# First up-projection panel of two convolution feed-forward layers: both tiles interleaved per plane, or one tile after the other

## The reference

```python
def conv_gated_ffn(h, w_up, conv_w, conv_b, w_down):
    a = h @ w_up                                   # 1024 -> 2 * 2816
    ap = jnp.pad(a, ((0, 0), (1, 1), (0, 0)))
    a = ap[:, :-2] * conv_w[0] + ap[:, 1:-1] * conv_w[1] + ap[:, 2:] * conv_w[2] + conv_b
    gate, val = a[..., :D_FF], a[..., D_FF:]
    return (jax.nn.silu(gate) * val) @ w_down

# in second_block, for l in range(2):
    x = x + memory_cross_attention(h, mem, ...)    # "mem"; its output product is followed by
    h = rms_norm_2(x, ffn_norm[l])                 # this norm, and then by
    x = x + conv_gated_ffn(h, ffn_w_up[l], ffn_conv_w[l], ffn_conv_b[l], ffn_w_down[l])   # "ffnc"
```

## Time and profile before

| | |
|---|---|
| median of 3 runs | 3700.81 us (3695.28 to 3701.74) |
| the profiled execution | 3697.01 us, its span 3695.2 us |
| PE busy | 3520.4 us, 95% of the span |
| DVE, ACT, POOL busy | 54%, 40%, 1% |
| chain that ended last | PE 87%, DVE 7%, ACT 2%, DMA 1% |

### The profile page before, as it was taken

How to read it: one execution, slowest core, us unless ns; L and a number is a source line. 1 busy time by engine, 2 the same in 40 slices (tenths; PEclk the granted TensorE clock), 3 DMA queues, 4 the chain that set the end, 5 groups by cost and what they waited for, 6 DMA issues and landing times.

```text
span 3695.2 us, 54759 instructions
## 1 busy us (share of the span) xinstructions
PE 3520.4 (95%) x21540; PEld 2923.2 (79%) x21540; DVE 1977.4 (54%) x2724; ACT 1474.0 (40%) x2212; POOL 20.6 (1%) x38
## 2 busy tenths in 40 slices
PE   7999995799999999999999999999999998989998
PEld 6888775678887888897778888778788896778887
DVE  4442469854434443335754424856677348557753
ACT  3332432243323332335643324655444247454432
POOL 0000000000000000000000000000000000000000
PEclk9999996699999999999999999999999999999999
DMA  3223220022232223222022233012233330222232
GB/s 121 96 95 97 77 74 9 2 80 96 96 94 83 96 96 96 82 91 75 18 80 96 95 97 93 30 40 83 90 100 94 96 97 13 69 81 91 96 98 90
DMA packets 84098, 296.08 MB, mean 80 GB/s; under 512 B 9504, under 2 KB 9504, under 8 KB 83680
## 3 DMA queue, kind: packets, MB, share of 16 engines
q1 hardware_dynamic: 82512, 288.24, 24.4%
q0 software_dynamic: 1424, 5.51, 0.5%
HBM read 291.61 MB, written 2.10 MB: 79 GB/s over the span
## 4 chain that ended last, share of the span: by engine, by line
PE 87%; DVE 7%; ACT 2%; issue 2%; DMA 1%; SPq 0%; DVEq 0%; ACTq 0%
PE PS L254 22%; PE PS L245 22%; PE PS L246 22%; PE PS L343 2%; PE PS L346 2%; PE PS L344 2%; PE PS L996 2%; PE PS L1007 1%; PE PS L1020 1%; PE PS L377 1%; DVE H_LO L470 1%; DVE WK L2556 1%; DVE WLO L221 1%; ACT WHI L217 1%; PE PS L384 1%
## 5 line engine op out<-in xcount | busy, mean ns | idle before, releaser
L245 PE MATMUL PS<-WK_R,WHI 128*128 128x512 f32 (+1 forms) x3680 | 1430.6, 389 | 16.4 <-DVE WLO L221 7.5
L246 PE MATMUL PS<-WK_R,WLO 128*128 128x512 f32 (+1 forms) x3680 | 1425.0, 388 | 0.0
L221 DVE TENSOR_TENSOR WLO<-RAW,WHI 128x1024 fp32r<-128x1024 f32 x563 | 689.0, 1224 | 1203.2 <-ACT WHI L217 1200.6
L217 ACT ACTIVATE WHI<-RAW 128x1024 fp32r<-128x1024 f32 x563 | 596.0, 1059 | 997.2 <-PE PS L254 822.3
L245 PEld LDWEIGHTS PS<-WK_R,WHI 128*128 128x128 f32 x3680 | 692.5, 188 | 168.6 <-issue 23.3
L246 PEld LDWEIGHTS PS<-WK_R,WLO 128*128 128x128 f32 x3680 | 692.5, 188 | 140.7 <-issue 0.7
L254 PE MATMUL PS<-H_LO,WHI 128*128 128x512 f32 x2680 | 673.1, 391 | 4.7 <-DVE H_LO L470 4.5
L254 PEld LDWEIGHTS PS<-H_LO,WHI 128*128 128x128 f32 x2680 | 502.0, 188 | 118.3 <-DVE H_LO L470 15.9
L254 PE MATMUL PS<-HID_LO,WHI 128*128 128x512 f32 x1056 | 263.2, 389 | 0.0
L254 PEld LDWEIGHTS PS<-HID_LO,WHI 128*128 128x128 f32 x1056 | 197.9, 188 | 40.9
L1188 DVE SCALAR_TENSOR_TENSOR SC<-SC,VEC 128x511 f32<-128x511 f32 x176 | 132.2, 751 | 110.5 <-ACT SC L1155 98.6
(11 more groups left out here) (378 smaller groups left out, 3559.0 us busy)
## 6 DMA issues: line engine op xcount, KB each, us to landing
RAW<-in_ffn_gu SPq DMA_DIRECT2D x176, 512.0 KB, 3.4
RAW<-in_f_up SPq DMA_DIRECT2D x88, 512.0 KB, 3.6
RAW<-in_ffn_dn SPq DMA_DIRECT2D x64, 512.0 KB, 3.5
RAW<-in_c_in SPq DMA_DIRECT2D x32, 512.0 KB, 3.4
RAW<-in_f_dn SPq DMA_DIRECT2D x32, 512.0 KB, 3.5
RAW<-in_ffn_dn SPq DMA_DIRECT2D x32, 384.0 KB, 3.1
RAW<-in_a_in SPq DMA_DIRECT2D x22, 512.0 KB, 3.5
RAW<-in_b_out SPq DMA_DIRECT2D x16, 512.0 KB, 3.6
```

The costliest lines, as they stand in the source:

```text
L217: nc.scalar.activation(WHI[:, slot, :], RAW[:, slot, :], ACT.Copy).then_inc(S("w_hi"), 1)
L221: nc.vector.tensor_tensor(WLO[:, slot, :], RAW[:, slot, :], WHI[:, slot, :].bitcast(F32), ALU.subtract).then_inc(S("w_lo"), 1)
L245: pe.matmul(o, WHI[:, slot, w], hi(k), start=(first and b_ == 0), stop=False)
L246: pe.matmul(o, WLO[:, slot, w], hi(k), start=False, stop=False)
```

## The change

For an early layer with two tiles, first_tiles now does the high products tile by tile. feature_hi of tile 0 waits for tile 0's weights alone and then for each plane. Both norm sums follow, and then feature_hi of tile 1 with its own wait. The low products and the spread behind them are as before. For all other calls nothing changes. The number of PE instructions is the same (6891 rows in both orders), and the queues of ACT, DVE, POOL and SP are the same.

```diff
             pe_bank(pe, p)
             apart = late(n)
-            pe.wait_ge(S("w_lo"), p.N + tiles)
-            for k in range(DT):
+            by_tile = early(n) and tiles > 1
+            if by_tile:
+                for i in range(tiles):
+                    feature_hi(pe, p, i, h_hi, range(DT), True, i, fresh=h_fresh(n))
+                    if i == 0:
+                        norm_add(pe, p, n, DT - 2)
+                        norm_add(pe, p, n, DT - 1)
+            else:
+                pe.wait_ge(S("w_lo"), p.N + tiles)
+            for k in () if by_tile else range(DT):
                 w = slice(128 * k, 128 * k + 128)
                 pe.wait_ge(S("norm_hi"), DT * n + k + 1)
                 for i in range(tiles):
```

## The result

The changed kernel took 3683.12 us, the median of 5 runs (3679.90 to 3685.41). The kernel before took 3700.81 us (5 runs, 3695.28 to 3703.41). The ratio is 0.9955, with a 95% interval of 0.9943 to 0.9966. So it is faster by 0.45%, some 17 us. 3683.5 us was predicted, with a range of 3677 to 3690.

What follows compares the result with a forecast made beforehand. The prediction took PE, busy 95% of the span, as the bound. Its terms of 9.44, 5.29 and 2.59 us sum to 17.32 us, taking the median of 3700.81 us to 3683.5 us, range 3677 to 3690 us.

Steps and rivals of the forecast that it cites:

- Start: First matmul at both seams: PE waits for tile 0's piece alone, 4.72 us earlier at each, 9.44 us.
- Clock: High products at both seams: with the gap short, PE stays at full clock, saving 2.76 and 2.53 us, 5.29 us.
- gap of 1.30 us: Idle time ahead of mem's output product: its window kept a clock of 1.00, the nearest row for the 5.29 us.
- Rival 1: Tile 0's start: the clock falls all the same, 12.0 us saved, 3688.8 us (one seam: 3686); chance 0.12.
- Low products: Tile 0's eight low products: earlier sum frees the reciprocal, so 1.82 us instead of 3.11 and 3.12, 2.59 us; chance not given.
- the covers: Slack before PE wants its operands: plane 7 1.3 us, tile 1's piece 0.7 us, low planes 0.5 us.
- Rival 3: Whole program: no change within 7.4 us, perhaps by second-layer mixb losing its clock, at most 1.7 us a window; chance 0.05.
- Rival 2: After tile 0's early start: PE stands before tile 1's piece or the low planes, 12.7 us left, 3688; chance 0.07.
- rival 4: Ahead of tile 1: late square of plane 7 and running sum hold PE up, slower, 3708.2 us or more; chance 0.02.

Runs made afterwards that it cites:

- wait for both: Changed kernel, but PE waits for both tiles' weights before tile 0's first product, as before the change; 3697.46 us against 3701.12 before, ratio 0.9993.
- busy gap: Kernel before, plus five unused products filling PE's gap ahead of its wait in the two layers; 3696.72 us against 3701.12 before, ratio 0.9993.
- sums late: Changed kernel, but both norm sums stand behind the high products of both tiles; 3689.69 us against 3701.12 before, ratio 0.9973.
- one seam: Changed kernel, with the new order in the first of the two layers only; 3693.36 us against 3700.59 before, ratio 0.9981.
- all layers: Changed kernel, with the four other feed-forwards' first panels tile by tile too, their sums unmoved; 3690.86 us against 3700.59 before, ratio 0.9973.
- late start: Changed kernel, but PE waits for the last plane's square before tile 0's first product; 3692.03 us against 3701.12 before, ratio 0.9982.
- reciprocal last: Kernel before, with VectorE's reciprocal behind all eight low planes at the two seams, not the fifth; 3699.98 us against 3700.23 before, ratio 0.9997.
- late, busy gap: Changed kernel with PE waiting for the last plane's square before tile 0, plus three unused products ahead; 3690.88 us against 3700.23 before, ratio 0.9972.

## Why the prediction was right

**Start.** 9.44 us were predicted and 9.99 measured: gaps of 0.39 and 0.63 us instead of 5.74 and 5.27. Waiting for both tiles brings the gap back, 5.07 us at the first seam. The forecast gaps were 1.02 and 0.55 us. The second was met. At the first, the odd execution is that of the kernel before, not that of the changed one: its ScalarE waited 1.91 us for tile 0's piece, where the wait is 1.27 us in the changed kernel and 1.24 us in "wait for both":

```profile
2594.85 1.06 ACT L217 ACTIVATE WHI<-RAW 128x1024 fp32r<-128x1024 f32 x1 [1.24 <-DMA RAW<-in_f_up]
```

The other kernels with an early start have first gaps of 0.27 to 0.37 us. So the 4.72 us a seam of the forecast are the repeatable term, and the 0.55 us above them are the late load of one execution, which is no gain of the change.

**Clock.** 5.29 us were predicted. The 32 high products took 7.47 and 7.44 us after, against 9.12 + 1.01 and 8.89 + 1.01 us before, so 2.66 + 2.46 = 5.12 us were saved. The busy gap shows it alone, and the windows show 1.00 through both seams. The forecast had only one gap of 1.30 us to go by, and gave the fall a chance of 0.12. The clock held at all seven early starts of four profiles (changed, "sums late", "one seam", "all layers"), behind gaps of 0.27 to 0.64 us. Rival 1 didn't come true at the gaps that were left (0.39 and 0.63 us). It would have at gaps of 3 us, as the late start shows: the row of 1.30 us was the right one to go by, but no proof for gaps much longer.

**Low products.** 2.59 us were predicted and 2.61 measured (1.81 us at each seam, from 3.11 and 3.12). Sums late brings the stall back, and reciprocal last removes it in the kernel before. The step's reason is shown, not only its size.

**Sums.** Not in the sum: both groups in a row take 1.70 us, where they took 1.61 apart (0.80 + 0.81). The forecast had the 1.7 us in its times of the covers, but left the difference out of the sum. That costs 0.18 us in all.

**Sum.** 9.99 + 5.12 + 2.61 - 0.18 = 17.54 us, which is what the seams give (9.22 + 8.32). The forecast was 17.32. Without the 0.55 us of the late load it is 17.0. That the total is met so closely is in part luck, since the interval of the ratio alone reaches from 12.6 to 21.1 us. But each term is met within 0.2 us, the late load apart, and that isn't luck. The span is 17.1 us shorter. The stretch ahead of the first seam was 1.17 us shorter in this execution, that between the seams 1.61 us longer, and that behind the second seam equal to 0.01 us.

**Rival 3 in small.** The 1.61 us are the clock further on, as the rival had it. Two windows of the second mixb were at full clock before and at half after. The first two rows are one place of mixb before and after, the windows are the changed kernel's:

```profile
3066.95 1.15 PE L1757 MATMUL PS<-CON,HID 128*96 128x128 f32 x8 [2.69 <-DVE HID_LO L2056]
...
3056.56 1.77 PE L1765 MATMUL PS<-CON,HID 128*96 128x128 f32 x8 [2.69 <-DVE HID_LO L2064]
...
3056.70:3060.10 3.40, 3.40 (x18) 3.34 (x17) 2.81 (x5) 1.49 (x3) 0.00 (x0) 0.50 0.02 5
3070.40:3073.80 3.40, 3.37 (x14) 2.39 (x14) 3.36 (x7) 1.43 (x4) 0.00 (x0) 0.50 0.00 0
```

The changed kernel is 10.39 us ahead at this place and 8.85 us ahead behind the first of the two windows, so that one alone costs 1.54 us. Whether it is the change's doing isn't shown. In the profiles of this study, the second mixb shows low clock for 0 us in the kernel before and in "late, busy gap", 3.4 us in "wait for both", "late start" and "reciprocal last", 6.8 us in the changed kernel, "sums late", "busy gap" and "one seam", and 10.2 us in "all layers". The four kernels whose seams are both under 15 us have 6.8, 6.8, 10.2 and 0 us, the four that wait for both tiles at both seams 0, 3.4, 3.4 and 6.8 us. With one profile of each that is no pattern and doesn't rule one out. Whether the changed kernel meets it more often than the one before stays open.

**Rival 2 and rival 4** did not come true. How near rival 2 was is shown by sums late: without the 1.7 us of sums between the tiles, PE waits 0.78 us for tile 1's weights. With them it doesn't wait.

## What to carry to other kernels

Ask for one operand at a time where the next layer begins: a wait for two buffers costs the arrival of the later one, although the first would feed the engine until then. Put the small work whose result another engine waits for into the time between the two, where it both starts that engine's chain sooner and covers the second arrival. The reverse holds where the activations come one by one and the weights are there: then interleave, so that each plane feeds as many products as it can and the clock is kept.

## What was unexpected

A gap of 2.85 and one of 3.26 us ahead of dense products lost the clock for 3.40 us in both seams of the late start, though nearly the same length (2.69 us) in the second mixb kept it in the kernel before. In the changed kernel the same 2.69 us gap stands ahead of a fall, the first of the two windows of rival 3. In the layers whose planes come 1.20 us apart, no gap among the products was over 0.47 us, and still the clock fell for 6.8 us in two layers of three. So the single short gaps at the seams (0.27 to 0.64 us) kept the clock each time, and repeated ones lost it twice in three times. The Trainium skill ("TensorE: Matmul & The Clock Gate", section "A second HAM failure mode: psum-queue depth-cycling") tells of another kernel in which PE's frequent micro-idles between groups of matmuls let the clock swing between its two levels. The trace of "all layers" agrees in two layers, with gaps of up to 0.47 us, and not in the third. No run here shows what decides between them.
